# Two softmax attentions of a hybrid layer stack: values as the stationary operand in two column halves, probabilities divided before they are turned

## The chip, the cores and the metric

One NeuronCore of one Trainium2 chip runs the whole program. The metric is the device time of one execution in microseconds. The profiles that are quoted here are of one execution each.

## The reference, cut to what matters

A sequence of 512 tokens of width 1024 goes through three layers in f32. The first layer mixes a banded attention, an mLSTM and a gated linear attention. The second layer ("fox") and the third (the latent one, "mla") each have an attention with 12 causal heads, a cross attention with 4 heads to 256 memory tokens, an output projection and a convolutional feed-forward of width 2816. The change touches these two attentions:

```
def causal_block_attention(q, k, v, log_decay=None):
    ...
        logits = jnp.einsum('bhqd,bhkd->bhqk', qc, k)
        if log_decay is not None:
            logits = logits + args[2][..., None] - log_decay[:, :, None, :]
        logits = jnp.where(key_idx[None, :] <= q_idx[:, None], logits, -jnp.inf)
        p = jax.nn.softmax(logits, axis=-1)
        return jnp.einsum('bhqk,bhkd->bhqd', p, v)

def memory_cross(qm, k_mem, v_mem, q_gain, k_gain):
    ...
    p = jax.nn.softmax(jnp.einsum('bshd,bmhd->bhsm', q, k), axis=-1)
    return jnp.einsum('bhsm,bmhd->bshd', p, v_mem).reshape(b, s, MEM_WIDTH)
...
    x = x + jnp.concatenate([o_mix, o_mem], axis=-1) @ w_out[i]
```

Heads are 64 wide; fox scores carry a decay, latent queries and keys are 96 wide (64 + 32 with rotary angles) and normed.

## The kernel before

Activations are kept feature-major (128 features on the partitions, 512 tokens in the free dimension). A dense product runs as three products of fp32r parts, high x high, high x low and low x high (`mm3`, lines 320 to 323). Weights are loaded in chunks by SP, their high part is made by ScalarE (line 302) and their low part by VectorE (line 312), both in time slots that `SCHEDULE`, `SPLITS` and `PIECES` (lines 2893 to 2955) write out. Every engine runs the same list of steps (`run`, line 2958): at a step it makes its share of the stage that is named there. So the order on each engine is fixed, and the engines wait for each other through counted events.

An attention (`class Attention`, line 989, with `pe_att`, `act_att`, `dve_att`) has 64 items, one for each head (4 memory heads, 12 others) and tile of 128 queries. An item has 128, 256, 384 or 512 keys for a causal head and 256 for a memory head. At step t:

- TensorE makes the scores of item t into a bank of ring S (4 banks in fox, 2 in the latent attention, 3 for its memory heads), in `score`, lines 1045 to 1070. Memory and fox heads are 64 rows deep, and the two heads of a pair are made together from the two row halves of the array; latent heads are 96 deep and made one at a time.
- VectorE takes the negative maximum of a row (line 1182). For latent heads ScalarE multiplies it by the query's norm factor (line 1138), and ScalarE makes the exponential with its row sum (line 1140) into a buffer P.
- Three steps later TensorE turns P in blocks of 128x128 (line 1077), and VectorE (or ScalarE for fox's memory heads) copies it out (lines 465, 460).
- Five steps later TensorE multiplies, with the turned block as the weights (128 columns) and 64 columns of values streaming, in plain f32 (line 1092). The result is token-major; a pair of heads fills one bank.
- When a pair is finished, VectorE makes reciprocals of the sums (line 1191) and multiplies the tiles into y (line 1197), TensorE turns y (line 1108), ScalarE makes the high part `hhi` (line 418) and VectorE the low part `hlo` (line 427), which the output projection reads.

Fox's items are ordered by `fox_order` (line 2230): two items of a memory tile stand before tile 0 of each of the six pairs, and two more before tile 2 of the first two. The latent attention has its memory heads first, and a head's four tiles in a row. Its stage is woven with the products that make its queries, keys and values in three groups (`pe_group` and so on, lines 2724 to 2856), whose rotary part and key norms are on GpSimd (`pool_group`, line 2813), and whose products use banks 3 and 7 for groups 0 and 1. GpSimd has no work in fox's attention. The tail: the output projection's first step comes three attention steps before the end, and its k part 5, the last pair's, is used last (`LATE`, line 2247).

## Time and profile before

| | |
|---|---|
| median of 3 runs | 1573.14 us (1569.53 to 1573.67) |
| profiled execution, its own time | 1568.96 us |
| its span, first to last instruction | 1567.2 us |
| TensorE busy | 1532.4 us, 98% (9018 matmuls) |
| VectorE, ScalarE, GpSimd busy | 824.6, 723.4, 317.8 us |
| fox attention, in the trace | 479.1 to 572.6 us |
| latent attention, in the trace | 1020 to 1150.8 us |

PE is TensorE's matmuls, PEld its weight loads, DVE VectorE, ACT ScalarE, POOL GpSimd. A group's row gives line, engine, operation, names (out<-in), rows * columns of weights and shapes, the count, then busy time in us and the mean of one in ns, then the engine's idle time before them in us and what ended it. Matmul records overlap each other, so the distance of their starts tells what one costs, not its duration. A row of the timeline has start, duration, engine, line and count of a run of like instructions.

### The profile page before, as it was taken

The page shows a single profiled execution, that of the slowest core. Times are in us where ns is not written, and L with a number is a line of the kernel's source. Part 1 is how long each engine was busy: PE and PEld are TensorE (multiplying, and loading weights), DVE is VectorE, ACT ScalarE, POOL GpSimd, SP SyncE. Part 2 cuts the span into 40 slices and gives each one's busy share as a digit, 9 for nine tenths or more (in the row PEclk, how much of TensorE's full clock was granted, in tenths as well). Part 3 has the DMA queues.
Part 4 walks back from the last instruction along what each step waited for, and adds up shares of the span by engine and source line. Part 5 has one row for each costly group of instructions (what it writes and reads, how often), then busy time and mean ns, then how long its engine had stood idle before and what let it go on. Part 6 is the DMA issues. An engine that isn't in the chain of part 4 may idle for free. (4 is left out here: it accounts for less than half of the span.)

```text
span 1567.2 us, 22136 instructions
## 1 busy us (share of the span) xinstructions
PE 1532.4 (98%) x9018; PEld 1288.9 (82%) x9018; DVE 824.6 (53%) x1405; ACT 723.4 (46%) x1402; POOL 317.8 (20%) x270
## 2 busy tenths in 40 slices
PE   7999998999999999999999999999999999999999
PEld 6888887998898887888888888668887888888887
DVE  5346556556435755745234443668956544244442
ACT  4346545455654544544124443567844443134431
POOL 0000142001430001344013431032001433024420
PEclk9999999999999999999999999999999999999999
DMA  6212112323220103233223332110022333223331
GB/s 234 75 41 88 54 55 89 129 68 108 78 89 27 39 1 108 82 107 119 90 79 102 100 111 75 48 44 14 16 66 81 105 97 122 80 81 98 114 111 41
DMA packets 37462, 128.07 MB, mean 82 GB/s; under 512 B 4192, under 2 KB 8944, under 8 KB 37360
## 3 DMA queue, kind: packets, MB, share of 16 engines
q1 hardware_dynamic: 37360, 126.65, 24.9%
q8 instruction: 71, 1.16, 0.3%
q14 instruction: 31, 0.25, 0.1%
HBM read 124.54 MB, written 2.10 MB: 81 GB/s over the span
## 5 line engine op out<-in xcount | busy, mean ns | idle before, releaser
L321 PE MATMUL bank<-hhi,whi 128*128 128x512 f32 (+2 forms) x1064 | 418.3, 393 | 2.8 <-ACT hhi L1936 1.8
L323 PE MATMUL bank<-hhi,wlo 128*128 128x512 f32 (+2 forms) x1064 | 414.4, 390 | 0.0
L322 PE MATMUL bank<-hlo,whi 128*128 128x512 f32 (+2 forms) x1064 | 414.2, 389 | 0.0
L312 DVE TENSOR_TENSOR wlo<-wstage,whi 128x1024 fp32r<-128x1024 f32 (+9 forms) x250 | 278.6, 1117 | 112.2 <-ACT whi L302 111.8
L302 ACT CAST whi<-wstage 128x1024 fp32r<-128x1024 f32 (+9 forms) x250 | 236.1, 949 | 135.6 <-PE bank L323 131.7
L2421 DVE SCALAR_TENSOR_TENSOR cr<-bank,vc,cr 128x511 f32<-128x511 f32 (+1 forms) x168 | 125.9, 749 | 217.1 <-ACT cr L2360 214.1
L321 PEld LDWEIGHTS bank<-hhi,whi 128*128 128x128 f32 (+2 forms) x1064 | 198.7, 187 | 49.3 <-ACT hhi L1936 4.3
L323 PEld LDWEIGHTS bank<-hhi,wlo 128*128 128x128 f32 (+2 forms) x1064 | 198.6, 187 | 43.2
L322 PEld LDWEIGHTS bank<-hlo,whi 128*128 128x128 f32 (+2 forms) x1064 | 198.7, 187 | 41.7 <-issue 0.5
L2360 ACT ACTIVATE cr<-bank,vc 128x512 f32<-128x512 f32 x84 | 65.5, 780 | 248.5 <-PE bank L323 246.1
L2466 POOL TENSOR_TENSOR cr<-cr,cr 128x512 f32<-128x512 f32 x44 | 94.4, 2146 | 315.4 <-DVE cr L2421 280.7
L321 PE MATMUL bank<-ahi,whi 128*128 128x512 f32 x352 | 137.8, 392 | 1.7 <-POOL alo L2472 1.7
L323 PE MATMUL bank<-ahi,wlo 128*128 128x512 f32 x352 | 137.1, 389 | 0.0
L322 PE MATMUL bank<-alo,whi 128*128 128x512 f32 x352 | 137.0, 389 | 0.0
L2472 POOL TENSOR_TENSOR alo<-cr,ahi 128x512 fp32r<-128x512 f32 x44 | 95.6, 2172 | 118.9 <-ACT ahi L2372 118.8
L321 PE MATMUL bank<-whi,hhi 128*128 128x384 f32 (+3 forms) x288 | 96.8, 336 | 1.5 <-issue 0.9
L322 PE MATMUL bank<-wlo,hhi 128*128 128x384 f32 (+3 forms) x288 | 94.1, 327 | 1.7 <-issue 1.7
L2445 DVE TENSOR_TENSOR xT<-bank,xT 128x512 f32<-128x512 f32 x32 | 22.1, 691 | 137.1 <-PE bank L323 137.1
L323 PE MATMUL bank<-whi,hlo 128*128 128x384 f32 (+3 forms) x288 | 94.1, 327 | 0.0
L321 PEld LDWEIGHTS bank<-ahi,whi 128*128 128x128 f32 x352 | 66.1, 188 | 16.7 <-issue 3.3
L323 PEld LDWEIGHTS bank<-ahi,wlo 128*128 128x128 f32 x352 | 66.1, 188 | 13.9
L322 PEld LDWEIGHTS bank<-alo,whi 128*128 128x128 f32 x352 | 66.1, 188 | 13.4
(412 smaller groups left out, 2298.5 us busy)
## 6 DMA issues: line engine op xcount, KB each, us to landing
wstage<-in_wts SPq DMA_DIRECT2D x147, 512.0 KB, 3.5
wstage<-in_wts SPq DMA_DIRECT2D x32, 704.0 KB, 4.0
wstage<-in_wts SPq DMA_DIRECT2D x14, 768.0 KB, 4.3
xT<-in_x SPq DMA_DIRECT2D x4, 512.0 KB, 5.3
xt<-in_x SPq DMA_DIRECT2D x4, 512.0 KB, 5.9
out<-ob SPq DMA_DIRECT2D x8, 256.0 KB, 2.3
U<-in_rel_ext SPq DMA_DIRECT2D x6, 256.0 KB, 9.0
wstage<-in_wts SPq DMA_DIRECT2D x2, 603.0 KB, 3.9
```

The costliest lines, as they stand in the source:

```text
L302: e.copy(K.whi[i % 3][:, p], K.stage[i % 3][:, p]).then_inc(*K.act.up(("whi", i, p.stop)))
L312: e.tensor_tensor(K.wlo[i % 3][:, p], K.stage[i % 3][:, p], K.whi[i % 3][:, p].bitcast(F32), SUB).then_inc(*K.dve.up(("wlo", i) if last el ...
L321: e.matmul(o, lh, rh, start=start, stop=False)
L322: e.matmul(o, lh, rl, start=False, stop=False)
L323: return e.matmul(o, ll, rh, start=False, stop=stop)
L2360: e.activation(t[:], divided(K, 1 + 2 * l, key) if first else K.bank(key)[:], ACT.Identity, scale=K.col(f"cw{l}", 3 * ch + 2), bias=K.col( ...
L2421: e.scalar_tensor_tensor(out=t[:, s:T], in0=b[:, 0:T - s], scalar=K.col(f"cw{l}", 3 * ch + 2 - s), in1=t[:, s:T], op0=MUL, op1=ADD).then_i ...
L2445: e.tensor_tensor(K.xT[:, m, :], K.bank((down, hv, m))[:], K.xT[:, m, :], ADD).then_inc(*K.dve.up(done, frees=[(down, hv, m)]))
L2466: e.tensor_tensor(g[:], g[:], v[:], MUL).then_inc(*K.pool.up(("gated", l, ch), frees=[((up, 22 + ch), "cr")]))
L2472: e.tensor_tensor(alo[:, ct, :], g[:], ahi[:, ct, :].bitcast(F32), SUB).then_inc(*K.pool.up(("alo", l, hv, ct), frees=[((up, 11 * hv + ct) ...
```

## The change

Both attentions get a class of their own, `TurnedAttention`, with `pe_turned`, `act_turned`, `dve_turned` and `pool_turned`; the first layer's attention keeps the old form.

- The exponentials are divided by their row sum before they are turned: VectorE makes the reciprocals of two items at a time, GpSimd multiplies P in place. The transposes are made five steps behind the scores, with seven buffers for P.
- The product with the values waits until both heads of a pair have their tile, at the seventh step after the later. The values (64 columns) are the weights, in column half 0 or 1 of the array by head, and the turned probabilities (128 queries) stream. The result is feature-major: head 0 in partitions 0 to 63 of the bank, head 1 in 64 to 127. y, its products and its transposes go.
- For latent heads GpSimd, not ScalarE, multiplies the maximum by the norm factor.
- Latent scores use three banks (0, 1, 7), but for items 16 to 23 two (0, 1). Outputs use one bank: 6 for both latent kinds and fox's memory heads, 7 for fox's others.
- `pool_group` makes its four key norms in four steps, not in one.
- `SCHEDULE` has one step more for each attention, the output projection begins one step earlier in it and has five attention steps before its second.

```diff
+class TurnedAttention(Attention):
+    TURN, VALUES = 5, 7
...
+        ends = {(p, i): max(t for t, (h, n) in enumerate(self.items) if (h // 2, n) == (p, i))
+                for p in range(len(heads) // 2) for i in range(4)}
+        self.ends = {t: tile for tile, t in ends.items()}
...
 def pe_turned(e, q, K, A):
...
     def turn(t):
         n = A.n(t)
         b = A.T.take(q, (A.name, "T", t))
-        q.wait_ge(*K.at((A.name, "P", t)))
+        q.wait_ge(*K.at((A.name, "divided", t)))
...
-    def pv(t):
-        h, i = A.items[t]
...
-            z = e.matmul(o, A.pt[A.name, "pt", t][:, j * P:(j + 1) * P], A.heads[h].v(j), start=j == 0, stop=j == n // P - 1)
-        z.then_inc(*K.pe.up((A.name, "pv", t), frees=[(A.name, "pt", t)]))
+    def values(p, i):
+        if i == 0:
+            (A.O4 if p < 2 else A.O).take(q, (A.name, "O", p))
+        for t, item in enumerate(A.items):
+            if item in ((2 * p, i), (2 * p + 1, i)):
+                q.wait_ge(*K.at((A.name, "pt", t)))
+        n = A.blocks(2 * p, i)
+        z = {}
+        for j in range(n):
...
+            for s in range(2):
+                o = K.bank((A.name, "O", p))[64 * s:64 * s + 64, i * P:(i + 1) * P]
+                z[s] = e.matmul(o, A.heads[2 * p + s].v(j), A.turned(p, i)[s][:, j, :], start=j == 0, stop=j == n - 1)
+        z[0].then_inc(*K.pe.up((A.name, "pv", p, i, "first")))
+        z[1].then_inc(*K.pe.up((A.name, "pv", p, i)))

     for t in A.steps:
...
-        if 3 <= t <= N + 2:
-            turn(t - 3)
-        if 5 <= t <= N + 4:
-            pv(t - 5)
-        p = A.post(t)
-        if p is not None:
-            q.wait_ge(*K.at((A.name, "fin", p)))
-            b = A.T.take(q, (A.name, "yT", p))
-            for c in range(4):
-                z = e.transpose(b[:, c * P:(c + 1) * P], A.y[A.name, "y", p][:, c, :], K.ident[:])
-            z.then_inc(*K.pe.up((A.name, "yT", p), frees=[(A.name, "y", p)]))
+        if t - A.VALUES in A.ends:
+            values(*A.ends[t - A.VALUES])
+        if 0 <= t - A.TURN < N:
+            turn(t - A.TURN)
...
-def act_att(e, q, K, A):
+def act_turned(e, q, K, A):
...
-            q.wait_ge(*K.at((A.name, "mx0", t)))
-            e.activation(m, m, ACT.Identity, scale=factor).then_inc(*K.act.up((A.name, "mx", t)))
         q.wait_ge(*K.at((A.name, "mx", t)))
...
-def dve_att(e, q, K, A):
+def dve_turned(e, q, K, A):
...
+        u = t - 3
+        if 0 <= u < N and u % 2 == 0:
+            q.wait_ge(*K.at((A.name, "P", u)))
+            q.wait_ge(*K.at((A.name, "P", u + 1)))
+            e.reciprocal(A.sums(u), A.sums(u)).then_inc(*K.dve.up((A.name, "rr", u)))
...
+def pool_turned(e, q, K, A):
+    N = len(A.items)
+    for t in A.steps:
+        u = t - 1
+        if 0 <= u < N and A.heads[A.items[u][0]].factor:
...
+            q.wait_ge(*K.at((A.name, "mx0", u)))
+            e.tensor_tensor(m, m, factor, MUL).then_inc(*K.pool.up((A.name, "mx", u)))
+        u = t - 3
+        if 0 <= u < N and u % 2 == 0:
+            q.wait_ge(*K.at((A.name, "rr", u)))
+            for item in (u, u + 1):
+                h, i = A.items[item]
+                p = A.P[A.name, "P", item][:, 0:A.n(item)]
+                e.tensor_scalar(p, p, A.rs[:, h, i:i + 1], None, MUL).then_inc(*K.pool.up((A.name, "divided", item)))
         yield
...
@@ pool_group
-    yield
-    for _ in range(3):
         yield
@@ schedule
-    out += ["fox", "foxatt", "foxatt"] * 5 + ["foxatt"] * 61
-    out += ["out0"] + ["foxatt"] * 3 + ["out0"] * 7 + ["bar5"] + ["norm1"] * 2 + ["ffn0"] * 63 + ["bar6"] + ["norm2"] * 2
+    out += ["fox", "foxatt", "foxatt"] * 5 + ["foxatt"] * 60
+    out += ["out0"] + ["foxatt"] * 5 + ["out0"] * 7 + ["bar5"] + ["norm1"] * 2 + ["ffn0"] * 63 + ["bar6"] + ["norm2"] * 2
...
-    for t in range(-2, 69):
+    for t in range(-2, 68):
...
@@ memory
+    K.RS4, K.RO6, K.RO7 = (Ring(K, b, K.in_bank) for b in ([*banks[0:2], banks[7]], banks[6:7], banks[7:8]))
...
-                K.foxatt = Attention("fox", mem_heads(K, 0, K.mqT) + fox_heads(K), (K.RS, K.RT, K.RO, None, K.RS), K.tmp, pt, None, sb("fox_mx", [P, 16, 4], scope=s3),
...
+                K.foxatt = TurnedAttention("fox", mem_heads(K, 0, K.mqT) + fox_heads(K), (K.RS, K.RT, K.RO7, None, K.RS, K.RS, K.RO6), probs,
...
-            K.mlaatt = Attention("mla", mem_heads(K, 1, K.mqT1) + mla_heads(K), (K.RS2, K.RT, K.RO, K.RQ, K.RS3), K.tmp, pt, None, sb("mla_mx", [P, 16, 4], scope=s2),
...
+            K.mlaatt = TurnedAttention("mla", mem_heads(K, 1, K.mqT1) + mla_heads(K), (K.RS4, K.RT, K.RO6, K.RQ, K.RS3, K.RS2, K.RO6), probs,
...
+                                       few=range(16, 24))
```

## Rows read from the trace of the kernel before

**Rows 1.** The page's first part: busy time of the engines.
```profile
PE 1532.4 (98%) x9018; PEld 1288.9 (82%) x9018; DVE 824.6 (53%) x1405; ACT 723.4 (46%) x1402; POOL 317.8 (20%) x270
```

**Rows 2.** Stretches of fox: length, busy PE, PEld, DVE, ACT, POOL; clock, DMA.
```profile
499.97:515.66 15.69, 15.35 (x145) 13.13 (x145) 11.75 (x34) 10.23 (x35) 0.00 (x0) 1.00 0.12 34
515.66:529.77 14.11, 13.99 (x134) 12.01 (x133) 12.05 (x35) 9.06 (x29) 0.00 (x0) 1.00 0.12 39
...
542.77:555.76 12.99, 12.95 (x130) 11.45 (x129) 9.05 (x25) 7.08 (x24) 0.00 (x0) 1.00 0.01 2
```

**Rows 3.** Stretches of the latent attention, same columns.
```profile
1020.00:1059.00 39.00, 35.42 (x206) 26.14 (x206) 27.18 (x76) 27.08 (x89) 13.63 (x18) 0.96 0.15 44
...
1108.13:1121.55 13.42, 13.25 (x116) 12.08 (x113) 12.31 (x30) 11.54 (x34) 0.00 (x0) 1.00 0.01 1
```

**Rows 4.** Waits in the latent attention: us in total, times, longest.
```profile
PEld bank L1051 <- ACT tmp L1140: 2.2, 5, 0.7
```

**Rows 5.** Groups of the whole trace: value products of fox's attention.
```profile
L1092 PE MATMUL bank<-fv,fox_pt 128*128 128x64 f32 x240 | 31.9, 265 | 0.0
...
L1092 PE MATMUL bank<-vmem,fox_pta 128*128 128x64 f32 x64 | 8.9, 262 | 0.0
```

**Rows 6.** Timeline of TensorE at the end of fox's attention.
```profile
562.68 0.61 PE L1108 MATMUL bank<-ident,y 128*128 128x128 f32 x4
563.13 0.38 PE L1077 MATMUL bank<-ident,tmp 128*128 128x128 f32 x2
...
570.25 2.57 PE L1092 MATMUL bank<-fv,fox_pt 128*128 128x64 f32 x22
...
572.94 0.40 PE L322 MATMUL bank<-hlo,whi 128*128 128x512 f32 x1
573.18 0.39 PE L323 MATMUL bank<-hhi,wlo 128*128 128x512 f32 x1
```

**Rows 7.** Timeline of TensorE in fox: value products, then scores of two heads.
```profile
531.77 1.00 PE L1092 MATMUL bank<-fv,fox_pt 128*128 128x64 f32 x8
532.70 0.39 PE L1051 MATMUL bank<-fkh,fqh 64*128 64x256 f32 x2
532.92 0.28 PE L1054 MATMUL bank<-fkl,fqh 64*128 64x256 f32 x2
533.04 0.29 PE L1057 MATMUL bank<-fkh,fql 64*128 64x256 f32 x2
```

**Rows 8.** Plain f32 products of 512 columns: four in the timeline, and their group.
```profile
1010.67 1.88 PE L2588 MATMUL bank<-tmp,ones 128*128 128x512 f32 x4
...
L2588 PE MATMUL bank<-tmp,ones 128*128 128x512 f32 x6 | 2.9, 591 | 0.0
```

**Rows 9.** Timeline: scores of two memory heads, then a transpose.
```profile
527.09 0.70 PE L1051 MATMUL bank<-kmg,mqT 64*128 64x256 f32 x4
527.72 0.55 PE L1077 MATMUL bank<-ident,tmp 128*128 128x128 f32 x3
```

**Rows 10.** Groups of VectorE: evacuation in fox; products y and reciprocals of the latent attention.
```profile
L465 DVE COPY fox_pt<-bank 128x512 f32<-128x512 f32 x12 | 8.2, 687 | 3.3 <-PE bank L1077 3.3
...
L1197 DVE TENSOR_TENSOR y<-bank,mla_rs 128x128 f32<-128x128 f32 x32 | 7.6, 282 | 0.3
...
L1191 DVE RECIPROCAL mla_rs<-mla_rs 128x8 f32<-128x8 f32 x8 | 1.6, 198 | 1.4 <-PE bank L1092 1.2
```

**Rows 11.** Groups of ScalarE: maxima scaled by the norm factor, exponentials of 512.
```profile
L1138 ACT ACTIVATE mla_mx<-mla_mx,r 128x1 f32<-128x1 f32 x48 | 14.0, 292 | 14.3 <-DVE mla_mx L1182 14.2
L1140 ACT ACTIVATE tmp<-bank,mla_mx,r 128x512 f32<-128x512 f32 x12 | 9.3, 777 | 0.4
```

**Rows 12.** Groups of GpSimd, whole trace.
```profile
L2472 POOL TENSOR_TENSOR alo<-cr,ahi 128x512 fp32r<-128x512 f32 x44 | 95.6, 2172 | 118.9 <-ACT ahi L2372 118.8
...
L1871 POOL TENSOR_TENSOR sum<-sum,tmp 128x512 f32<-128x512 f32 x10 | 13.0, 1300 | 41.3 <-ACT tmp L1835 41.3
...
L2822 POOL COPY kt<-krr 128x512 f32<-128x512 f32 x3 | 1.8, 611 | 51.3 <-DVE krr L2703 51.2
```

More of the change, by code:

```diff
@@ L1042, in pe_att, with turned_to @@
+def turned_to(A, q, K, t):
+    h, i = A.items[t]
+    if A.before[h // 2, i] is not None:
+        q.wait_ge(*K.at((A.name, "pv", *A.before[h // 2, i])))
+    else:
+        for event in A.free_after:
+            q.wait_ge(*K.at(event))
+    n = A.blocks(h, i)
+    return A.turned(h // 2, i)[h % 2], K.bank((A.name, "T", t))[:, 0:n * P].rearrange("p (j n) -> p j n", j=n)
 def pe_att(e, q, K, A):
@@ L1045, in score @@
     def score(ts):
-        at = [(t, A.items[t][1], A.heads[A.items[t][0]], A.n(t), (A.S4 if A.items[t][0] < 4 else A.S).take(q, (A.name, "S", t))) for t in ts]
+        at = [(t, A.items[t][1], A.heads[A.items[t][0]], A.n(t), A.S.take(q, (A.name, "S", t))) for t in ts]
+        z = {}
+        for t, i, H, n, b in at:
+            for r in H.ready:
+                q.wait_ge(*K.at(r))
+            z[t] = e.matmul(b[:, 0:n], H.q(i), H.k(n), start=True, stop=False)
+        for t, i, H, n, b in at:
+            e.matmul(b[:, 0:n], H.q(i), H.low(i, n)[1], start=False, stop=False)
@@ L1047, in score, with pe_turned @@
+def pe_turned(e, q, K, A):
+    N = len(A.items)
+    def score(ts):
+        at = [(t, A.items[t][1], A.heads[A.items[t][0]], A.n(t), A.scores(t).take(q, (A.name, "S", t))) for t in ts]
         z = {}
@@ L1200, in dve_att @@
[L1200 to L1211 removed]
+        q.wait_ge(*K.at((A.name, "S", t)))
```

272 lines of the change are left out of this document (171 added, 101 removed).

## The prediction, made before the changed kernel had run

> **What bounds the kernel now.** Start with the page's first part [rows 1]: TensorE (PE) is busy in 98% of the 1567.2 us span, so what counts is TensorE's order of work, stage by stage. The change touches two stages: the fox attention (479.1 to 572.6 us of the trace, 93.5 us) and the latent one (1020 to 1150.8 us, 130.8 us). I cut both at the starts of head pairs and read the busy times of every engine there. In the fox stage PE is busy in 12.95 of 12.99 us in a steady pair, VectorE (DVE) 9.05, ScalarE (ACT) 7.08, GpSimd (POOL) 0 [rows 2]: TensorE is the bound. In two earlier windows DVE has 11.75 of 15.69 and 12.05 of 14.11 us, close behind. In the latent stage a steady pair lasts 13.42 us with PE 13.25, DVE 12.31, ACT 11.54 [rows 3]: PE again, with DVE 1.1 us behind it. There the list of waits also has TensorE waiting for a score bank that ACT still reads, 2.2 us in 5 waits [rows 4].
>
> **Values as weights.** Today every block of turned probabilities (128 keys x 128 queries) is loaded as weights and 64 columns of values stream past: 240 + 64 instructions per attention, the same counts in both [rows 5], two per block since plain f32 takes two. Their busy times overlap, so the price is the distance of their starts: 22 in a row are busy for 2.57 us and one alone for 0.265, so (2.57 - 0.27) / 21 = 0.110 us [rows 5, 6]. They stream 64 columns. In f32 four instructions of 512 columns are busy for 1.88 us and one for 0.59, (1.88 - 0.59) / 3 = 0.43 us each [rows 8]; 64 columns would take 0.054. So 0.110 is the load of 128 weight columns. After the change 64 columns of values are the weights, and 128 queries stream: 0.107 us an instruction at 0.43 per 512. If the two heads of a pair, in the two column halves, run side by side, one such time serves two instructions. The count stays: 2 x 304 = 608. Saving 608 x 0.110 / 2 = 33.4 us, 16.7 per attention. That column halves run side by side is not in this trace. Row halves are: two matmuls of the same line for two heads together take 0.12 us (533.04 after 532.92) [rows 7], half of the 0.24 that one of 512 columns takes on the full array (573.18 after 572.94) [rows 6]; and so for f32 too, where four of 256 columns took 0.63 us, not 4 x 0.214 [rows 9]. I take side by side, the nearest row; the other bound is no overlap, a saving of 608 x 0.003, nothing.
>
> **Output transposes.** Outputs now come feature-major, so the transposes of y go: four for each of 8 pairs in two attentions, 64. Four took 563.13 - 562.68 = 0.45 us [rows 6]. 64 x 0.11 = 7.0 us off TensorE.
>
> **Switches of the array's shape.** Where fox goes from full array to row halves, eight value products take 0.93 us, 0.05 more than 8 x 0.110, and the first score of 256 columns takes 0.22 us against 0.12 for the next [rows 7]: 0.15 us for a switch. The memory heads' four matmuls show 0.63 against two rounds of 0.214, 0.20 for entry and exit, 0.10 each [rows 9]. Bounds 0 and 0.20, I take 0.12. The change puts one group of column-half products between scores and transposes per pair and tile: in fox rows-columns-full in place of rows-full, one more switch, 32; in the latent stage one more for 8 memory tiles and two for 24 others, 56. 88 x 0.12 = 10.6 us back (0 to 17.6).
> Here the Trainium skill speaks against the change ("TensorEngine Tiling (Array Packing)", Key Properties): changing the tiling mode drains the engine. It gives no price; the rows' 0.10 to 0.15 us agree with a drain, and by that rule the 88 switches cost something for sure, so the bound of 0 would go.
>
> **TensorE in all:** 33.4 + 7.0 - 10.6 = 29.8 us less work, 16.4 in fox, 13.5 in the latent stage.
>
> **DVE.** Off: per attention 32 products y, busy for 7.6 us, and 8 reciprocals, 1.6 us [rows 10], 9.2 us. On: 32 reciprocals of two columns; the nearest row has eight columns and 0.20 us, so 0.10 to 0.20, I take 0.18, 5.8 us. Net -3.4 us, 0.4 a pair. The casts hidden in the stage and the evacuations stay.
> **ACT.** The 48 scalings of the maximum, 14.0 us [rows 11], go to POOL. Nothing else changes but places.
> **POOL.** New: 64 divisions per attention, 12 x 1280 + 16 x 256 = 19,456 columns. Bounds: the 512-column copy, 0.611 us (1.19 ns a column, 23 us); the two-input product next to DVE work, 2.172 us (4.24 ns, 83 us); between them the two-input product with DVE less busy, 1.300 us (49 us) [rows 12]. A division by a per-partition scalar reads one tensor, so I take 0.65 us for 512, 25 us in a stage of 80 us or more: hidden behind TensorE. If that cover goes (rival C) it is a new bound. Scaling the maximum: between nothing and the copy's 0.611 us, and I take the 0.292 that ACT needs for it [rows 11]; it stands on the path from maximum to exponential, and waits behind up to two divisions (1.2 us) queued on POOL. The k norms of the latent groups, on POOL too, are now spread over four steps so that they hold up divisions by one product each.
> **What is late next.** Turning at five steps and values at seven give the new chain exponential, reciprocal, two divisions, transpose two steps (2.4 to 3 us) more than before. It needs 0.2 + 2 x 0.65 us plus queues: it fits. Third score bank: the score-maximum-exponential loop of a latent item gets three steps for what had two; it may give back the 2.2 us of [rows 4]. Single output banks: in fox a memory tile lies between pairs, so high and low copies have three steps; fine. At each stage's end the last transposes and last value products now stand next to each other with one evacuation (0.69 us [rows 10]) between: +0.9 us, twice; today the value products of three earlier items still follow the last transposes: 22 stand in a row there [rows 6]. Weight loads and SP keep their order; foxatt and mlaatt steps move by one, covered by the output projection.
>
> **The sum by stage.** Fox: 16.4 off TensorE. In the two windows near DVE's line TensorE would need 15.7 - 2.7 = 13.0 and 14.1 - 2.7 = 11.4 us, DVE without a gap 11.4 and 11.7; for the waits there I take 2.5 us, and 0.9 at the end: -13. Latent: a steady pair would be 13.4 - 2.2 (products) - 0.4 (y) + 8 x 0.12 = 11.7 us for TensorE, but DVE holds 12.3 - 0.4 = 11.9 us with no gap, so 12.2: -1.2 for each of six pairs, -1 of the first 39 us (PE busy 35.42, ACT and POOL chains in it [rows 3]), +0.9 at the end, +1 for POOL's place in the chain: -6. Together -19. The profiled execution took 1568.96 us, 1.8 more than its span, and 4.2 less than the median of the runs, 1573.14. So 1550 against its own time, and 1554 against the median.
>
> **Rivals** (all against the median).
> A, better: switches cost nothing and the third bank frees the latent stage: 29.8 + 10.6 on TensorE, cut by DVE's line, about -29: 1544. For it: DVE's new load. Against: [rows 7, 9]. 0.08.
> B, slower: the column halves don't run side by side. Each value instruction then holds the array for 0.107 us where it held it 0.110: -1.8, transposes -7.0, switches +10.6, ends +1.8, POOL's place +1: +4.6, 1578; with switches at 0.20, 1585. It decides at the value products: with over 0.100 us between their starts the sum, 608 x (0.110 - x) + 7.0 - 10.6 - 2.8, is negative. For it: no row shows column halves, and the two instructions of one f32 product could block the other head's. Against: row halves do it with f32 [rows 9]. 0.16.
> C: POOL becomes the bound. A fox pair with its memory tiles is 2560 + 683 columns; at 4.24 ns that is 13.7 us against the 13.0 of today, so TensorE's gain is lost there, and a latent pair is 10.9 + 8 x 0.29 = 13.2 us against 13.4: about 1574. It decides above 4.0 ns a column. For it: POOL's products took 2.172 us in the feed-forward. Against: those read two tensors. 0.08.
> The Trainium skill ("GPSIMD Engine Reference", When to use GPSIMD, Engine selection) would keep elementwise work on VectorE as GpSimd is about half as fast with two inputs, but calls one input roughly line rate. By that C falls; no row here shows a one-input product on POOL.
> D: the latent chain exponential, reciprocal, two divisions, maximum, exponential closes over two steps. With an exponential of 0.78 us [rows 11] and its sum, 0.18, 1.2, 0.29 and what the queues add it needs some 2.9 us against 3.0 for two steps of 12.2 / 8; if it binds, the latent stage gains nothing: fox -13, total -12, 1561. 0.16.
>
> **How the numbers follow.** Forecast 0.52, A 0.08, B 0.16, C 0.08, D 0.16. Time: the forecast's, 1554. Its own range, by the bounds of the switches and DVE's line, is 1547 to 1562. With D and C, and B's lower part, 1544 to 1577 leaves out some 0.17. A measurement of this kernel tells 0.3% (4.7 us) from no change. Faster: forecast, A, D, 0.76. Same: most of C and the mild end of B, 0.10. Slower: the rest, 0.14.
>
> **What would show it.** Value products in pairs that start within 0.02 us of each other, and some 0.055 us an instruction: forecast right, B wrong. Fox pairs of about 10.5 to 11 us and latent pairs of 12. The first matmul after a value group later by 0.1 us: the switch price. POOL products of 512 columns near 0.65 us; at 1.3 the stage still holds, at 2 C. ACT waiting for mla_mx from POOL by over 20 us in all: D. If the value instructions lie 0.107 us apart, or TensorE's idle time grows by over 15 us in the stages, the prediction is wrong.

## The result, and the profile after

The changed kernel takes 1610.14 us (median of 4 runs, 1608.97 to 1612.17), the kernel before took 1571.34 us beside it (4 runs, 1565.97 to 1573.67). The ratio is 1.0253, with a 95% interval of 1.0223 to 1.0284: slower by about 39 us, where 19 us less were forecast; the range that was given ended at 1577. The profiled execution of the changed kernel has a span of 1609.0 us, that of the kernel before 1567.2.

The page's first part, after the change, against [rows 1]:

```profile
span 1609.0 us, 22166 instructions
PE 1534.8 (95%) x8954; PEld 1263.9 (79%) x8954; DVE 818.8 (51%) x1389; ACT 709.4 (44%) x1354; POOL 458.2 (28%) x446
```

TensorE has fewer instructions, yet it is busy no shorter. Is that the value products? Their groups in the fox stage answer to [rows 5]; "xcount | busy us, mean ns" stand at the end of each line:

```profile
L1265 PE MATMUL bank<-fox_pt,fv 128*64 128x128 f32 x240 | 18.4, 282 | 2.1 <-DVE fox_pt L465 2.1
...
L1265 PE MATMUL bank<-fox_ptm,vmem 128*64 128x128 f32 x64 | 5.3, 285 | 0.0
```

It isn't: they are busy for 18.4 + 5.3 us where 31.9 + 8.9 stood. Sixteen of them in a row take 1.09 us at the full clock (the timeline of the fox end further down has such a row), so (1.09 - 0.27) / 15 = 0.055 us an instruction, half of the 0.110 of before. The two instructions of a pair start 7 ns apart. The column halves do run side by side, and the mechanism of the largest term was right.

To see where the time went I compared the starts of the same dense matmul (lines 321 to 323) in both traces. Between two of them on either side of a stage the difference grows by what the stage lost. Outside the attentions it moves by up to 5 us from one profiled execution to another; inside, five stages hold it all: the fox attention between its last dense matmul and the first piece of the output projection ("fox"), the first 24 matmuls of that piece, with the last attention work between them ("fox end"), the first latent heads with the groups' work ("latent first"), the latent heads after them ("latent steady", 61.1 us before), and the first 23 matmuls of the latent output piece ("latent end"). The changed kernel lost 4.0, 5.2, 6.9, 19.8 and 3.9 us there, 39.8 in all. Every such number is of the one profiled execution of its kernel, and can differ from the median of the runs: in two of the kernels further down (1588.80 and 1584.37 us) the profiled execution took 6 us less than the median.

The windows of the two long stages, first in the kernel before, then in the changed one; the columns are length, busy time and count by engine, then the granted TensorE clock as a share of 2.4 GHz:

```profile
core 0: us, PE busy (x) PEld busy (x) DVE busy (x) ACT busy (x) POOL busy (x), PEclk, DMA share, GB/s
489.05:572.62 83.57, 82.23 (x788) 71.55 (x788) 60.95 (x163) 47.14 (x154) 0.00 (x0) 1.00 0.06 20
1089.66:1150.76 61.10, 58.85 (x490) 53.04 (x489) 53.87 (x130) 49.90 (x145) 3.34 (x4) 1.00 0.09 27
```

```profile
491.34:578.92 87.58, 70.18 (x731) 48.84 (x730) 56.72 (x157) 46.84 (x155) 63.66 (x62) 0.99 0.06 19
1107.88:1188.75 80.87, 63.61 (x447) 49.17 (x446) 52.98 (x128) 42.43 (x115) 51.27 (x80) 0.82 0.06 18
```

In the fox stage TensorE's work fell by 12 us, and its idle time grew from 1.3 to 17.4. In the latent stage it idles for 17.3 us instead of 2.3, and although it has less to do it is busy for 4.8 us more, at a granted clock of 0.82 of full speed instead of 1.00. So stalls can cost twice: once as a wait, once as a lower clock for the work behind it. In the fox stage, with as much idle time, they did not: its clock is 0.99.

What GpSimd's new instructions cost shows in their groups in the latent attention:

```profile
L1378 POOL TENSOR_SCALAR tmp<-tmp,mla_rs 128x256 f32<-128x256 f32 x21 | 19.3, 924 | 1.8 <-DVE mla_rs L1353 1.8
L1378 POOL TENSOR_SCALAR tmp<-tmp,mla_rs 128x512 f32<-128x512 f32 x8 | 12.7, 1586 | 0.0
...
L1371 POOL TENSOR_TENSOR mla_mx<-mla_mx,r 128x1 f32<-128x1 f32 x48 | 8.7, 190 | 14.7 <-DVE mla_mx L1333 13.7 <-ACT mla_p L1300 1.0
```

A division of 512 columns takes 1.59 us (1.56 to 1.76 in the 24 of both attentions) where the forecast took 0.65; from 256 to 512 columns it is (1.586 - 0.924) / 256 = 2.6 ns a column. The Trainium skill ("GPSIMD Engine Reference", When to use GPSIMD, Engine selection) has one-input work at roughly line rate; this case's one-input product is much nearer to the two-input ones of [rows 12], and the measurement decides.

The list of waits in the latent stage of the changed kernel, from 1110.5 us on (us in total, times, longest):

```profile
ACT tmp L1300 <- POOL mla_mx L1371: 23.8, 14, 3.3
POOL tmp L1378 <- DVE mla_rs L1353: 12.1, 11, 1.6
...
ACT mla_p L1300 <- POOL mla_mx L1371: 7.5, 4, 2.8
DVE hlo L427 <- ACT hhi L1322: 6.6, 5, 2.2
PE bank L1247 <- POOL tmp L1378: 6.0, 7, 1.5
```

The first line, with the third, is the sign that the prediction named for its rival D: ScalarE waits over 20 us for maxima from GpSimd (23.8 + 7.5 = 31.3). One turn of the loop, from the timeline ("start us, us"; in brackets the idle time before, and what ended it):

```profile
1135.97 0.40 DVE L1333 TENSOR_REDUCE mla_mx<-bank 128x1 f32<-128x256 f32 x1
1136.15 2.97 POOL L1378 TENSOR_SCALAR tmp<-tmp,mla_rs 128x384 f32<-128x384 f32 x2 [1.63 <-DVE mla_rs L1353]
...
1139.10 0.33 POOL L1371 TENSOR_TENSOR mla_mx<-mla_mx,r 128x1 f32<-128x1 f32 x2
1139.31 0.56 ACT L1300 ACTIVATE mla_p<-bank,mla_mx,r 128x256 f32<-128x256 f32 x1 [2.81 <-POOL mla_mx L1371]
...
1140.00 0.17 DVE L1353 RECIPROCAL mla_rs<-mla_rs 128x2 f32<-128x2 f32 x1 [1.06 <-ACT mla_p L1300]
```

The maximum is reduced at 1136.37, but GpSimd works on two divisions until 1139.1, scales it only then, and the exponential starts 2.9 us late. VectorE, in its turn, stands in its reciprocal and waits for that exponential. In the fox stage there is no scaling, and the loop is another (the same view):

```profile
502.53 0.15 DVE L1353 RECIPROCAL fox_rs<-fox_rs 128x2 f32<-128x2 f32 x1
...
502.78 3.12 POOL L1378 TENSOR_SCALAR tmp<-tmp,fox_rs 128x512 f32<-128x512 f32 x2 [0.58 <-DVE fox_rs L1353]
...
505.15 0.69 DVE L465 COPY fox_pt<-bank 128x512 f32<-128x512 f32 x1 [0.48 <-PE bank L1247]
505.76 0.16 DVE L1353 RECIPROCAL fox_rs<-fox_rs 128x2 f32<-128x2 f32 x1
...
507.29 0.69 DVE L465 COPY fox_pt<-bank 128x512 f32<-128x512 f32 x1 [1.19 <-PE bank L1247]
...
508.56 0.16 DVE L1353 RECIPROCAL fox_rs<-fox_rs 128x2 f32<-128x2 f32 x1
```

The reciprocal of a pair stands on VectorE behind an evacuation, which waits for a turn, which waits for a division, which needed an earlier reciprocal.

One rival can be read off the same trace: that VectorE and GpSimd, both at work in SBUF now, lengthen each other's instructions. In both attentions together VectorE's instructions that took over 0.1 us more than the median of their line and shape took 2.6 us more in all, GpSimd's 0.9 us. That is not where 39 us went.

### The profile page after: what moved, and what is told of

Read it like the earlier page. It is cut to its first block and busy times, and to the rows that moved or that the text cites. A ratio compares the mean times of both kernels' runs of the same rounds, so it can differ in the third digit from the quotient of the medians.

```text
span 1609.0 us, 22166 instructions
## 1 busy us (share of the span) xinstructions
PE 1534.8 (95%) x8954; PEld 1263.9 (79%) x8954; DVE 818.8 (51%) x1389; ACT 709.4 (44%) x1354; POOL 458.2 (28%) x446
## 5 line engine op out<-in xcount | busy, mean ns | idle before, releaser
L321 PEld LDWEIGHTS bank<-ahi,whi 128*128 128x128 f32 x352 | 66.1, 188 | 16.7 <-issue 3.3
```

Of the source, the lines that this page charges most:

```text
L321: e.matmul(o, lh, rh, start=start, stop=False)
```

## Experiments: is it GpSimd's price?

The first theory was that GpSimd's price is the whole loss, through these loops. Four kernels, each one edit on the changed kernel. The first takes the price away and keeps the order:

```
-                p = A.P[A.name, "P", item][:, 0:A.n(item)]
+                p = A.P[A.name, "P", item][:, 0:1]
```

> The division touches only the first of the 128 to 512 columns of each probability tile (the other columns stay undivided; all waits and the order of the instructions stay), so GpSimd's 1.57 us for 512 columns falls to about 0.3 us. Theory (the loops through GpSimd's 2.5 ns a column are the whole loss, and the parts on TensorE are worth what the prediction gave them): about 1552 us, between 1545 and 1560, fox pairs of 11 to 12 us instead of 13.7, latent pairs of 12 to 13 us instead of 17 to 19. Rival 1 (the new order itself, turning at five steps' distance and values behind it, is what stalls): above 1598 us, within 12 us of the changed kernel. Rival 2 (the distance costs half and the division half): 1570 to 1585.

Measured: 1590.22 us (1587.17 to 1594.87), ratio to the kernel before 1.0127 [1.0096, 1.0159]. By stage it stands at -2.5, +4.7, +2.4, +11.0 and +5.0 against the kernel before. So 20 of the 39 us go with the price, and 19 us of loss remain in which no division takes longer than 0.31 us. Theory and rivals all missed: something else holds up the latent stage.

The second puts the scaling of the maxima back (on ScalarE, 0.29 us each):

```
+        if A.heads[h].factor:
+            q.wait_ge(*K.at((A.name, "mx0", t)))
+            e.activation(m, m, ACT.Identity, scale=factor).then_inc(*K.act.up((A.name, "mx", t)))
```

> The scaling of the latent maxima (16 of 0.19 us) goes back from GpSimd to ScalarE, where the kernel before had it; the divisions stay. Theory (in the latent attention a maximum queues behind two divisions on GpSimd, up to 3.0 us, and the exponential behind it closes the loop): latent pairs fall from 17.2-18.8 us to about 14, the total by 12 to 22 us to 1588-1598; the fox attention is unchanged at 13.7 us a pair. Rival 1 (GpSimd's divisions hold the probabilities back, whoever scales the maxima): within 4 us of 1610. Rival 2 (all the loss of the latent attention is this queue, and its gain shows as well): 1570-1580.

Measured: 1604.25 us (1601.94 to 1605.37), ratio 1.0212 [1.0185, 1.0240]. The latent steady stage fell from +19.8 to +13.6, the fox stage stayed at +4.0, as expected. The queue is real but worth 6 us, not 12 to 22, and none of the three ranges holds it. (The scalings are 48, not the 16 of the expectation.)

The third moves the reciprocal ahead of the evacuation in VectorE's step:

```
+        u = t - 3
+        if 0 <= u < N and u % 2 == 0:
+            ... e.reciprocal(A.sums(u), A.sums(u)) ...
         u = t - A.TURN
         if 0 <= u < N and not A.turned_on_act(u):
             dve_evac(...)
```

> On VectorE the reciprocal of a pair of items goes ahead of the evacuation of the turned item five steps back, in the same step. Theory (in the fox attention the reciprocal stands behind an evacuation that waits for a turn, that waits for a division, that waits for the reciprocal before: a loop of 13.7 us a pair): fox pairs fall to 12.0-13.2 us, the total by 3 to 9 us; the latent attention, whose loop runs through the maxima on GpSimd, moves by under 3 us. Rival 1 (GpSimd's own busy time, 11 of 13.7 us a pair with its fixed gaps, bounds the pair): within 2 us of 1610. Rival 2 (the evacuation, now behind the reciprocal's wait for the exponential, is late instead): slower by 2 to 8 us.

Measured: 1597.76 us (1592.28 to 1599.47), ratio 1.0167 [1.0135, 1.0199]: 12 us faster, more than expected, and in another place. The fox stage stands at +6.0, no better; the first latent heads went from +6.9 to +2.3 and the latent steady stage from +19.8 to +12.2. The place of the reciprocal matters, but my account of where did not hold: the loop that I read in the fox stage was not what cost the 12 us.

The fourth gives all divisions to VectorE:

```
+            for item in (u, u + 1):
+                q.wait_ge(*K.at((A.name, "rr", u)))
+                e.tensor_scalar(p, p, A.rs[:, h, i:i + 1], None, MUL).then_inc(*K.dve.up((A.name, "divided", item)))
```

> All 48 divisions go from GpSimd to VectorE, each right behind the reciprocal of its pair; the scaling of the maxima stays on GpSimd. Estimate: 512 columns of f32 in SBUF take VectorE 0.3 to 0.6 us, so 9 to 19 us of work an attention in all. Theory (GpSimd's price and the queue on it are the loss): 1550 to 1568 us, faster than the kernel before. Rival 1 (VectorE, at 12.3 of 13.4 us a latent pair before, becomes the bound with the divisions on it): 1570 to 1590, latent pairs of 14 us or more with VectorE over 95% busy. Rival 2 (the order at five steps' distance is the loss): above 1598.

Measured: 1607.36 us (1603.54 to 1611.06), ratio 1.0230 [1.0192, 1.0268], although a division is cheap there:

```profile
L1359 DVE TENSOR_SCALAR tmp<-tmp,fox_rs 128x256 f32<-128x256 f32 x19 | 6.1, 350 | 0.3
L1359 DVE TENSOR_SCALAR tmp<-tmp,fox_rs 128x512 f32<-128x512 f32 x10 | 4.5, 483 | 0.2
```

At 0.48 us instead of 1.59 for 512 columns next to nothing is gained (all 64 divisions of each attention moved, not the 48 of the expectation), and the theory and both rivals missed. The stages stand at +3.8, +4.0, +10.6, +12.5 and +4.9: the first latent heads lost more than before. The trace shows a part of that. Eleven of the 64 latent divisions took 0.83 to 1.09 us where others of their width take 0.29 to 0.42, 6.8 us more in all. Each of them ran beside a two-input product of GpSimd, and ended 0.08 to 0.22 us after it; in the fox attention, where GpSimd is idle, there is none. GpSimd's price alone is not the cause; the first theory falls, by the 19 us that are left with the narrow division.

## Experiments: distance or order?

The second theory was VectorE's program order: it waits in the reciprocal for an exponential of the step before, and a longer distance should let both of its waits end early. The edit, on top of the reciprocal ahead of the evacuation (the output pieces keep their place):

```
-        u = t - 3
+        u = t - 4
-    TURN, VALUES = 5, 7
+    TURN, VALUES = 6, 8
```

> Reciprocal of a pair and its divisions one step later (four steps behind the pair's first scores instead of three), the reciprocal ahead of the evacuation, the turn at six steps instead of five and the values at eight instead of seven; GpSimd divides all columns. Theory 2 (VectorE's program order is the loop: it waits in the reciprocal for an exponential whose maximum it reduced one step before, and in the evacuation for a division; with a step more between them both waits end early): against the kernel with the reciprocal ahead alone (1598) faster by 8 to 20 us, 1578 to 1590, the latent steady part (61 us before the change, 78 after) at 64 to 70. Rival 1 (GpSimd's 2.5 ns a column bound the pair at this distance too): 1594 to 1602. Rival 2 (a longer distance only lengthens the ends): 1600 to 1606.

> The same order as the kernel with all a step later, and the division on the first column of each tile only (the rest of the columns stays undivided). Against the narrow division at the old distance (1590): theory 2 (the waits of VectorE for an exponential of the step before are what is left there, and TensorE's clock falls with them): 1555 to 1572, TensorE's granted clock back over 0.95 in the latent steady part. Rival 1 (what is left are one bank for two turned items and one bank for the outputs): 1585 to 1595. Rival 2 (maxima by way of GpSimd, a third engine between VectorE and ScalarE): 1578 to 1590.

> All a step later as above, GpSimd divides all columns, and the scaling of the latent maxima goes back to ScalarE. Theory 2 with the queue on GpSimd as a second loop: 6 to 12 us below the kernel with all a step later alone, 1570 to 1582. Rival 1 (with the distance longer the maximum no longer meets the divisions on GpSimd): the same within 3 us. Rival 2 (ScalarE's 0.3 us for each scaling makes it the bound of the latent part): slower by 2 to 6 us.

> Reciprocal, divisions, turn and values a step later, the maxima scaled on ScalarE and all divisions on VectorE: GpSimd does nothing in either attention. Theory 2: no loop is left but VectorE's own work; VectorE's busy time in the latent steady part, 53.8 of 61.1 us before the change, less the output scaling and plus about 9 us of divisions, is 55 to 60 us: 1560 to 1572, and the first of these kernels at or under the kernel before. Rival 1 (VectorE is the bound at over 95% busy and holds TensorE's clock down): 1575 to 1590. Rival 2 (the ends and the switches of shape lose what the values gain): 1572 to 1578.

Measured: 1597.86 us (1597.55 to 1598.32) for the step alone, 1588.80 (1579.63 to 1596.73) with the narrow division, 1601.11 (1598.97 to 1603.27) with the maxima on ScalarE, 1614.08 (1610.05 to 1617.20) with the divisions on VectorE too. The fox stage answers: -2.6 instead of +6.0 at GpSimd's full price, so there the distance does cure. The latent steady stage does not: +15.8, +6.4, +16.0 and +16.3. The second theory holds for one attention of two. Of the four totals the first two fall in the range of a rival and not of the theory, the third is 3 us above the first where the theory had it 6 to 12 below (its second rival's range), and the fourth missed every range. In this fourth kernel 15 latent divisions took longer beside GpSimd's work, 8.6 us in all.

What is left in the latent stage shows in the timeline of the narrow one, where the division costs nothing:

```profile
1113.21 0.54 DVE L465 COPY mla_pt<-bank 128x384 f32<-128x384 f32 x1
...
1114.35 0.67 ACT L1316 ACTIVATE mqh<-bank,gq 96x512 fp32r<-96x512 f32 x1
...
1114.92 0.57 ACT L1322 CAST hhi<-bank 128x512 fp32r<-128x512 f32 x1
...
1115.53 0.69 DVE L427 TENSOR_TENSOR hlo<-bank,hhi 128x512 fp32r<-128x512 f32 x1 [1.78 <-ACT hhi L1322]
1116.13 0.28 DVE L1333 TENSOR_REDUCE mla_mx<-bank 128x1 f32<-128x128 f32 x1
1116.33 0.68 DVE L465 COPY mla_pt<-bank 128x512 f32<-128x512 f32 x1
...
1117.07 0.44 PE L1247 MATMUL bank<-ident,tmp 128*128 128x128 f32 x2 [1.42 <-DVE mla_pt L465]
```

VectorE is done at 1113.75 and the next maximum is ready to be reduced, but the next instruction in its order is the low part of the outputs, and that waits for ScalarE's high part. In the kernel before the low part stood one step behind the high part and ahead of the evacuation; the change moved it into the same step. The third theory: this is a third wait (behind the queue for the maxima and the wait in the reciprocal), and the three hide one another. The edit, in VectorE's step:

```
         if 1 <= t < N + 1:
             soft(t - 1)
+        p = A.done(t - A.VALUES - 2)
+        if p is not None:
+            dve_lo(...)
...
-        p = A.done(t - A.VALUES - 1)
-        if p is not None:
-            dve_lo(...)
```

> VectorE forms the low part of a pair's outputs (hlo) one step later and ahead of the evacuation, as it stood in the kernel before, instead of in the step in which ScalarE forms the high part; all else as in the changed kernel. Theory 3 (VectorE waits about 1 to 1.8 us for ScalarE's copy at each pair of heads, the maxima queue behind it, TensorE idles and its granted clock falls): faster than 1610 by 6 to 14 us, most of it in the latent steady part, the wait of the low part for the high part under 2 us in an attention. Rival (the wait only takes the place of the waits for GpSimd's divisions): within 4 us.

> The low part a step later and ahead of the evacuation, and reciprocal, divisions, turn and values a step later too (1598 without the first of these); GpSimd divides all columns. Theory 3: 1580 to 1590. Rival (GpSimd, whose divisions and maxima queue on each other in the latent part, is the bound): 1593 to 1600.

> The same with the division on the first column of each tile only (the rest stays undivided). Theory 3 (the price of the divisions, the two waits of VectorE and the order at the ends are together the whole loss): 1558 to 1572, granted clock over 0.95 in the latent steady part. Rival 1 (the path of the maxima by way of GpSimd still stalls it): 1575 to 1585. Rival 2 (nothing gained on the same kernel without the low part moved): 1585 to 1590.

> The turn stays at five steps; the low part a step later and ahead of the evacuation, the reciprocal ahead of the evacuation, the latent maxima scaled on ScalarE; GpSimd divides all columns. Theory 3: each of the three takes one wait away, 1580 to 1590. Rival (with the divisions at 2.5 ns a column the turn at five steps is late whatever the rest): 1592 to 1600.

Measured: alone 1602.97 us (1600.48 to 1603.19), 7 us faster, within the expectation. With all a step later 1593.32 (1592.71 to 1596.17), the rival's range. That with the narrow division 1579.94 (1576.62 to 1582.84), the first rival's range; its latent steady stage stands at +1.9, that of the kernel before it at +12.5. And with the reciprocal ahead and the maxima on ScalarE, at the old distance and GpSimd's full price, 1576.56 (1574.34 to 1582.44), ratio 1.0030 [1.0017, 1.0044], 3 us better than the theory's range. One at a time the low part, the reciprocal and the maxima bring 7.2, 12.4 and 5.9 us, 25.4 in sum before rounding; together they bring 33.6. The windows of that kernel, the two stages and the two ends:

```profile
489.74:571.28 81.54, 70.09 (x731) 48.95 (x730) 57.47 (x157) 46.12 (x155) 63.60 (x62) 0.99 0.07 21
1094.45:1154.40 59.95, 51.67 (x447) 40.90 (x446) 51.18 (x127) 49.60 (x145) 42.54 (x43) 0.99 0.08 22
571.28:582.79 11.51, 10.63 (x58) 8.21 (x57) 1.38 (x2) 0.59 (x1) 0.66 (x1) 0.78 0.00 0
1154.40:1164.07 9.67, 9.67 (x65) 7.42 (x64) 1.25 (x2) 0.35 (x1) 0.94 (x1) 0.88 0.09 36
```

The latent steady stage is 59.95 us long instead of 80.87. Of the 20.9 us between them 11.9 are TensorE's busy time (63.61 against 51.67, with 447 instructions both times): by an estimate that is the clock but for about 1 us, as 51.67 x 0.99 / 0.82 = 62.4. The other 9.0 are idle time. This splits the time of the stage and is no price: whether TensorE at the full clock would only have waited longer there, no run tells. ScalarE's wait for the maxima there is down to 7.7 us (6.6 and one of 1.1):

```profile
ACT mla_mx L1304 <- DVE mla_mx L1339: 6.6, 9, 1.5
...
DVE hlo L427 <- ACT hhi L1328: 2.1, 4, 0.6
```

## Experiments: what is left

On the kernel with the three edits: one edit taken out, the division made narrow, the first output piece moved, the distance lengthened. The piece moves by this edit (and likewise for the latent one):

```
-    out += ["fox", "foxatt", "foxatt"] * 5 + ["foxatt"] * 60
-    out += ["out0"] + ["foxatt"] * 5 + ["out0"] * 7 + ...
+    out += ["fox", "foxatt", "foxatt"] * 5 + ["foxatt"] * 61
+    out += ["out0"] + ["foxatt"] * 4 + ["out0"] * 7 + ...
```

> The low part a step later and the latent maxima on ScalarE, the reciprocal behind the evacuation as in the changed kernel; GpSimd divides all columns, the turn stays at five steps. Against the kernel with all three edits (1577): theory 3 (three separate waits, each of which alone keeps TensorE waiting and its clock low): slower by 5 to 12 us, 1582 to 1589. Rival (the reciprocal's place does nothing once the other two are out): within 3 us of 1577.

> The three edits (low part a step later, reciprocal ahead of the evacuation, maxima on ScalarE), and the division on the first column of each tile only (the other columns stay undivided). This prices GpSimd's 2.5 ns a column in an order without the other waits. Theory 3: 1564 to 1571, so 6 to 12 us of the whole loss are the division's real price. Rival 1 (the price is hidden once the order is right): within 3 us of 1577. Rival 2 (the division alone stands between the change and the forecast): 1550 to 1560.

> The three edits, and the first 21 or so dense matmuls of the output projection one step later in both attentions, behind the turn of the last probabilities instead of ahead of it, so that the last evacuation lies beside them. Theory (at each end the turn, its evacuation and the last products come one after another behind the dense piece, about 2 us of them bare): faster than 1577 by 2 to 5 us. Rival (the wait for GpSimd's last divisions, 1.6 us each, comes ahead of the piece then and takes the gain): within 2 us, or slower.

> The three edits, and reciprocal, divisions, turn and values all a step later (turn at six). Theory: the fox attention gains 2 to 4 us as it did before, the latent one nothing, 1571 to 1577. Rival (a step more makes the latent one lose, as it did without these edits): 1580 to 1595.

Measured: 1588.31 us (1585.59 to 1593.66) with the reciprocal back behind the evacuation, so its place is worth 11.8 us even with the other two made, as much as alone (12.4), and within the theory's range. What hides one another is then the other two: the low part and the maxima bring 7.2 and 5.9 us alone, 13.1 in sum, and 21.8 together. Leaving out one of these two was not run. 1569.36 (1563.27 to 1571.41) with the narrow division, ratio 0.9982 [0.9969, 0.9996]: GpSimd's price is worth 7.2 us in an order without the three waits, 4.2 of them in the fox stage, and only there does the reordered change come out ahead of the kernel before, by 2 us, with its divisions left out. This is within the theory's range too. 1575.63 (1572.18 to 1577.10) with the pieces later: the fox end goes from +5.5 to +0.8 and the fox stage from -2.0 to -0.7, in the latent attention the gain of 1.5 at the end is given back ahead of it, and the median moved by only 0.9 us, within the runs' spread and as the rival said. 1592.55 (1588.86 to 1594.03) with all a step later: the fox stage gains 1.8 us, the latent steady stage loses 15.8; the total is in the rival's range. The step brings the high part of the outputs into the same step as the cast of a head's queries, behind which it stands in the timeline above. This is not shown to be the reason, and it can't be the whole: the kernel with the low part and all else a step later has the same two casts in one step, and stands at +12.5 in that stage with the full divisions and at +1.9 with the narrow ones. So at the longer distance GpSimd's price counts again; the rest is open.

At the ends the order counts, and the clock. The end of the fox attention with the three edits:

```profile
578.63 0.88 PE L1265 MATMUL bank<-fox_pt,fv 128*64 128x128 f32 x12
...
579.44 0.66 PE L1247 MATMUL bank<-ident,tmp 128*128 128x128 f32 x4
580.13 0.69 DVE L465 COPY fox_pt<-bank 128x512 f32<-128x512 f32 x1 [7.77 <-PE bank L1247]
...
580.97 1.09 PE L1265 MATMUL bank<-fox_pt,fv 128*64 128x128 f32 x16 [0.88 <-DVE fox_pt L465]
```

The last turn, its evacuation and the last products stand behind the 21 dense matmuls of the piece, one after another, 0.9 us of it with TensorE idle. Ahead of the piece TensorE has waited (in the changed kernel it is busy for 2.23 of the 4.00 us from 575 to 579), and the piece starts at the lower level, 1.2 GHz; in the changed kernel, two windows of the same kind of matmul:

```profile
579.00:582.90 3.90, 3.90 (x11) 3.04 (x10) 0.69 (x1) 0.00 (x0) 0.57 (x1) 0.50 0.00 0
583.50:585.50 2.00, 2.00 (x11) 1.63 (x10) 0.00 (x0) 0.00 (x0) 0.00 (x0) 1.00 0.00 0
```

At 0.50 of full speed the starts of the dense matmuls lie 0.43 us apart, at 1.00 0.23; the first ten cost 2 us more.

The last two kernels put the findings together: the three edits, the first output piece of the fox attention a step later, and the division of the fox attention split by width; the second also has the longer distance there alone:

```
+                if A.name == "fox" and A.n(item) >= 384:
+                    e.tensor_scalar(p, p, A.rs[:, h, i:i + 1], None, MUL).then_inc(*K.dve.up((A.name, "divided", item)))
...
+        self.TURN, self.VALUES = (6, 8) if name == "fox" else (5, 7)
```

> The three edits in both attentions; in the fox attention alone also the first output piece a step later, and the divisions of tiles of 384 and 512 columns on VectorE (0.48 us for 512 columns in the kernel with all divisions there) while GpSimd keeps those of 128 and 256; the latent attention as with the three edits. From the stages of the earlier runs: 1577, less 3.4 for the piece in the fox attention and less 3 to 4 for the dear divisions: 1568 to 1572, level with the kernel before or up to 0.3% faster. Rival (VectorE, with 11 us more of work in the fox attention, holds the maxima back): 1573 to 1578.

> The same, and in the fox attention alone reciprocal, divisions, turn and values a step later (turn at six; the latent one stays at five, where a step more cost it 15 us). The step gave the fox attention 1.8 us in its steady part and 1.5 at its end before: 1565 to 1570. Rival (distance and the cheaper division take the same wait away): the same as the kernel at five steps within 2 us.

Measured: 1584.37 us (1578.74 to 1587.61) for the split, worse than its own rival: the fox stage is at +6.4, where the kernel with the piece moved had -0.7. VectorE is busy for 66.4 us there instead of 58.2, at a granted clock of TensorE of 0.91 instead of 0.98. VectorE's load alone is not the reason: with the longer distance it is busy for 64.7 us, and the fox stage is back at -0.6. That kernel takes 1574.52 us (1570.20 to 1579.63), ratio 1.0018 [1.0006, 1.0030], above its forecast of 1565 to 1570, and its rival, within 2 us of the split at five steps, missed too. It has the lowest median of the complete versions, 1 us under the one with the piece moved, which the runs' spread does not tell apart, and it is still 0.1 to 0.3% slower than the kernel before. No version that computes everything beat it.

## Why the prediction was wrong

By stage the forecast had -13 us for the fox attention and -6 for the latent one; measured are +9.2 and +30.6. The step that failed is "It needs 0.2 + 2 x 0.65 us plus queues: it fits", with the small terms for waits that hang on it (2.5 us in fox, +1 for GpSimd's place, +0.9 us at each end). TensorE's work did fall, but its idle time grew by 16.1 us in the fox stage and by 15.0 in the latent one, and the prediction named over 15 us as the sign that it is wrong. Three moved instructions account for 33.6 of the 39 us of loss, the price of the divisions for 7.2 more in the order without them.

**Right.** The value products run in pairs side by side at 0.055 us each; rival B is out. The transposes of the outputs went. The scaling of the maximum on GpSimd takes 0.19 us (0.29 taken), the reciprocal 0.15 to 0.17 (0.18 taken). A switch of the array's shape costs near what was taken, as shown below.

**Wrong: "so I take 0.65 us for 512".** It is 1.59, between the bounds of [rows 12] and above the middle one, 1.300. The argument from the number of inputs was all that stood for the low end. The bounds were in the text, but rival C was priced only against GpSimd's busy time, and by that it stays out: GpSimd is busy for 63.7 of 87.6 us and 51.3 of 80.9, never the bound. The price is worth 7 us in a good order and 20 in the changed one.

**Wrong: "It needs 0.2 + 2 x 0.65 us plus queues: it fits".** This counted the chain of one item and not what VectorE has behind each wait. The reciprocal was costed at its 0.18 us of work; what it costs is that it stands between an evacuation and the next maximum, waiting for another engine: 12 us by its place alone, shown twice (1610 to 1598, 1588 to 1577).

**Wrong: "high and low copies have three steps; fine".** That looked at the bank and not at VectorE. The low part, moved into the high part's step, costs 7 us alone.

**Too small: "+1 for POOL's place in the chain".** It is 6 us alone. Rival D named this loop and its sign, and the sign came (31.3 us of waiting in the steady stage), but D priced it with 0.65 us a division and took "the latent stage gains nothing" as its worst. The attention also lost 31 us, which this loop does not explain: the reciprocal's place costs 12 by itself, and of the queue for the maxima and the wait for the high part one hides the other, so that taking away both brings 9 us more than the sum of each alone.

**Missing: the clock.** Every term of the sum stood at the granted clock of 1.00. In the latent steady stage some 11 of 20.9 us lie in it. A forecast that lets TensorE idle where it did not idle before needs that term, with 0 as its other bound: the fox stage idled as long and kept 0.99.

**Near, for fox: "88 x 0.12".** A busy time counts neighbours that overlap twice over, so I gave each TensorE instruction of fox and its end the time from its start to the next one's start, or to its own end where it stood alone:

```
                          before   changed   three edits, narrow
value products (304)       34.4      21.4      21.4 us
turns of P (150 and 152)   18.6      25.7      24.6
transposes of y (32)        4.0       -         -
scores and bias            25.3      25.3      25.2
```

Products at 0.055 us would take 16.7 us; they take 21.4, in every version. The 4.7 us between them are 32 groups at 0.15, where the forecast had 3.8 at 0.12. One switch can be read in the timeline of the fox end above: twelve products from 578.63 at 0.055 put the last one at 579.24, and the turn behind it starts at 579.44, 0.20 us later. In the changed kernel this distance is 0.20 us in all 31 places where a turn follows a group, and inside a group it is 0.10 from the second instruction of a pair to the first of the next. This agrees with the rule that a change of the tiling mode drains the engine (the Trainium skill, "TensorEngine Tiling (Array Packing)", Key Properties); no run separates a drain from other reasons.

The turns take 6 to 7 us more, but this is no price of the new switches. Some 2.7 us changed only their row: in the kernel before, the switch to the row halves of the scores stood behind value products (0.205 us to the first score in 25 places), now it stands behind turns (0.202 in 20). Some 4 us in the changed kernel, 2 in the narrow one, are turns with idle time behind them, 27 and 21 of them, which count with their whole 0.27 us. With such records set at the distance of their neighbours on both sides, TensorE's saving in fox is an estimated 12.5 to 13 us, and not 16.4; the 2.5 to 3 us that the switches do not explain were not taken apart, nor the switches of the latent attention.

**Too small: "+0.9 us, twice"** for the ends. They cost 5.2 and 3.9 us, and about 5.5 and 3.9 with the three edits; moving one piece took 3.4 of these from the fox attention.

With the three edits and the narrow division the two steady stages stand at -6.3 and -2.4 us. TensorE has 69.1 us of work in 77.3 there and 52.0 in 58.8, VectorE 55.3 and 51.2: neither fills its stage alone, and what holds the other 8.2 and 6.7 us was not taken apart. The banks, of which the expectations name the one for the outputs and the one for turned items, are a rival for it that no run tried. "DVE without a gap", on which the forecast's sum rests, was never reached.

## What to carry to other kernels

When work moves to a new engine, or an instruction to a new step, write down for each engine's program what stands behind every wait, and who waits for that: here three instructions of 0.15 to 0.7 us, well priced as work, cost 7, 12 and 6 us by their places alone, and 34 together. Take out one at a time and then all: a wait that hides behind another shows only so. Take the high end for an operation that the trace does not show on that engine. And where TensorE has been busy without a gap, price a stall twice, once as idle time and once as the lower clock after it, the second between nothing and what the latent stage shows here.

## What the runs showed of the hardware

- Two plain f32 products in the two column halves run side by side, 0.055 us an instruction instead of 0.110; a group of them between scores and transposes costs some 0.15 us more than its products (4.7 us for 32 groups), and a turn behind it starts 0.20 us after its last product.
- A product of f32 by a per-partition scalar, in place in SBUF: GpSimd 0.92 us for 256 columns and 1.59 for 512, 0.28 for one column; VectorE 0.35 and 0.48.
- Such a product on VectorE that ran beside a two-input product of GpSimd (256 or 384 columns, 0.73 to 0.84 us) ended 0.08 to 0.22 us after it: 11 of 64 in the latent attention, up to 1.09 us long.
- The granted clock was 0.50 of full speed from 579.0 to 582.9, behind 4 us in which TensorE was busy for 2.23, and 1.00 again from 583.5, behind dense matmuls. Over a stage with 17 us of idle time in 81 it was 0.82, over one with 8 us in 60 it was 0.99, and over the fox stage, with 17 us in 88, it was 0.99 too: the sum of idle time does not tell it.
